# Light expert units loaded behind the next heavy block's units, light stages spaced unevenly, and a small copy moved on

## What is computed

```
def _swiglu(h, w_gate, w_up, w_down):
    return (jax.nn.silu(h @ w_gate) * (h @ w_up)) @ w_down

def _moe(h, router, w_gate, w_up, w_down):
    logits = (xf @ router).astype(jnp.float32)
    top_logits, top_idx = lax.top_k(logits, TOP_K)
    gates = jax.nn.softmax(top_logits, axis=-1)
    ...  # each expert: _swiglu of its tokens, with w_gate[e], w_up[e], w_down[e]
    ...  # the results, times their gates, are summed by token
```

## Time and profile before

| what | value |
|---|---|
| median of 3 runs | 1554.77 us (1552.6 to 1555.14) |
| profiled execution: time, span in the trace | 1556.36 us, 1554.6 us |
| busy time in the span: PE, DVE, ACT, POOL | 95%, 58%, 47%, 20% |
| DMA: bytes, mean rate over the span | 469.61 MB, 302 GB/s |
| rate in the slices of the MoE | mostly 350 to 409 GB/s |

### The profile page before, as it was taken

One profiled execution on the slowest core, in us unless ns is written; L12 is line 12 of the kernel. 1 busy time (PEld: TensorE's weight loads), 2 busy tenths in 40 slices (PEclk: granted clock), 3 DMA queues, 4 the chain that ended last, 5 costly groups with the idle time before them and its releaser, 6 DMA issues.

```text
span 1554.6 us, 22445 instructions
## 1 busy us (share of the span) xinstructions
PE 1482.5 (95%) x9550; PEld 1138.3 (73%) x9550; DVE 907.6 (58%) x665; ACT 731.7 (47%) x588; POOL 303.4 (20%) x295
## 2 busy tenths in 40 slices
PE   9999999999999999999999999999998999999997
PEld 8887889999988788876565565666655666656675
DVE  5555566655567748865454555554554545545687
ACT  5444445433355356753444445444444444444565
POOL 5599225300035205840000000000000000000100
PEclk9999999999999999999999999999999999999999
DMA  9544548765521186998999999999999999999994
GB/s 346 177 163 162 190 158 290 275 214 181 186 79 57 44 321 225 374 381 354 406 370 407 361 392 409 371 398 397 382 392 379 409 349 385 395 376 396 390 381 160
DMA packets 141598, 469.61 MB, mean 302 GB/s; under 512 B 8649, under 2 KB 21153, under 8 KB 129201
## 3 DMA queue, kind: packets, MB, share of 16 engines
q1 hardware_dynamic: 137424, 454.58, 77.3%
q0 software_dynamic: 3920, 13.44, 2.6%
q10 hardware_dynamic: 144, 0.07, 0.0%
HBM read 462.02 MB, written 15.21 MB: 307 GB/s over the span
## 4 chain that ended last, share of the span: by engine, by line
PE 66%; DMA 16%; DVE 8%; ACT 7%; issue 2%; POOL 1%; SPq 0%; ACTq 0%; DVEq 0%; POOLq 0%
PE PS L2037 64%; DMA weights_raw<-in_moe_w_up 6%; DMA weights_raw<-in_moe_w_down 6%; ACT weights_hi L1111 6%; DVE weights_lo L1531 6%; DMA weights_raw<-in_moe_w_gate 3%; PE PS L2252 1%; POOL b_padded L929 1%; PE PS L2451 0%; ACT c_padded L1111 0%; DVE act_rows L1531 0%; DVE residual L1531 0%; POOL param_tmp L788 0%; DMA constants<-in_constants 0%; DVE small_act_rows L1531 0%
## 5 line engine op out<-in xcount | busy, mean ns | idle before, releaser
L1531 DVE TENSOR_TENSOR weights_lo<-weights_raw,weights_hi 128x2048 fp32r<-128x2048 f32 (+2 forms) x323 | 680.0, 2114 | 527.7 <-ACT weights_hi L1111 526.4
L1111 ACT ACTIVATE weights_hi<-weights_raw 128x2048 fp32r<-128x2048 f32 (+2 forms) x323 | 564.0, 1752 | 576.3 <-PE PS L2037 218.7
L2037 PE MATMUL PS<-weights_hi,gathered_hi 128*128 128x512 f32 (+1 forms) x640 | 241.8, 378 | 33.6 <-DVE weights_lo L1531 33.0
L2037 PE MATMUL PS<-weights_lo,gathered_hi 128*128 128x512 f32 (+1 forms) x640 | 234.2, 366 | 0.0
L2037 PE MATMUL PS<-weights_hi,gathered_lo 128*128 128x512 f32 (+1 forms) x640 | 234.1, 366 | 0.0
L2037 PE MATMUL PS<-weights_hi,act_transposed_hi 128*128 128x512 f32 x456 | 187.8, 412 | 13.5 <-DVE weights_lo L1531 13.4
L2037 PEld LDWEIGHTS PS<-weights_hi,gathered_hi 128*128 128x128 f32 x640 | 120.1, 188 | 88.8 <-issue 40.9
L2037 PE MATMUL PS<-x_transposed_hi,weights_hi 128*128 128x256 f32 x640 | 181.2, 283 | 1.3 <-DVE weights_lo L1531 1.1
L2037 PE MATMUL PS<-weights_hi,act_transposed_lo 128*128 128x512 f32 x456 | 181.6, 398 | 0.0
L2037 PE MATMUL PS<-weights_lo,act_transposed_hi 128*128 128x512 f32 x456 | 181.5, 398 | 0.0
L2037 PE MATMUL PS<-x_transposed_lo,weights_hi 128*128 128x256 f32 x640 | 179.7, 281 | 0.0
(11 more groups left out here) (330 smaller groups left out, 1453.8 us busy)
## 6 DMA issues: line engine op xcount, KB each, us to landing
weights_raw<-in_moe_w_up SPq DMA_DIRECT2D x127, 896.0 KB, 9.0
weights_raw<-in_moe_w_gate SPq DMA_DIRECT2D x125, 896.0 KB, 8.8
weights_raw<-in_moe_w_down SPq DMA_DIRECT2D x96, 1024.0 KB, 8.1
weights_raw<-in_ret_w_in SPq DMA_DIRECT2D x24, 1024.0 KB, 6.7
weights_raw<-in_moe_w_down SPq DMA_DIRECT2D x32, 512.0 KB, 7.7
weights_raw<-in_ffn_w_gate SPq DMA_DIRECT2D x14, 1024.0 KB, 5.1
weights_raw<-in_ffn_w_up SPq DMA_DIRECT2D x14, 1024.0 KB, 5.0
weights_raw<-in_ffn_w_down SPq DMA_DIRECT2D x14, 1024.0 KB, 4.9
```

Source lines behind the costliest of these rows:

```text
L1111: return nc.scalar.activation(o, i, ACT.Copy)
L1531: return nc.vector.tensor_tensor(o, a, b, op)
L2037: return nc.tensor.matmul(o, l, r, start=start, stop=stop)
```

## The change

`small_after` now reads a table in which each light stage has its own places: four blocks behind four heavy blocks in a row, one heavy block with none, then the two down blocks. Behind every second stage there is one more heavy block with none. `units_in_order` takes the number of blocks by which light units are loaded behind their place of use: 1 for loading (`ORDER`, `NUMBER`), 0 for use (`USED_ORDER`). In the load order the units of the light block of place k now follow those of heavy block k + 1; TensorE still uses them ahead of that heavy block. `done_at(n)` gives the value of `used` at which load number n was used, and takes the place of `n + 1` in all waits on `used` in the MoE. On ScalarE the copy to `act_t_small` leaves `after_small` for `after_small_turn`, which runs at l = 2k + 6 instead of 2k + 4.

```
-    turn, at = divmod(k - START, 5)
-    j = 4 * turn + at
-    return j if at < 4 and 0 <= j < len(LIGHT) * len(BLOCKS) else None
+def small_positions():
+    after, k = {}, START
+    for stage in range(len(LIGHT) * ESTEPS):
+        for at in range(6):
+            after[k] = 6 * stage + at
+            k += 2 if at == 3 else 1
+        k += stage % 2
+    return after
...
-def units_in_order():
+def units_in_order(behind):
...
-        for ranks, at in ((WHOLE, k), (LIGHT, small_after(k))):
+        for ranks, at in ((WHOLE, k), (LIGHT, small_after(k - behind))):
...
+ORDER = units_in_order(1)
+USED_ORDER = units_in_order(0)
+DONE = {NUMBER[of]: MOE_U0 + m + 1 for m, of in enumerate(USED_ORDER)}
+def done_at(n):
+    return DONE.get(n, n + 1)
...
 (SP, load)
-                            sp.wait_ge(used, last + 1)
+                            sp.wait_ge(used, done_at(last))
...
 (ScalarE, split_hi)
-                    act.wait_ge(used, count(SPLIT_UNITS[SPLIT_NUMBER[n] - SPLIT] + 1, e, EXPERT_UNITS))
+                    act.wait_ge(used, count(done_at(SPLIT_UNITS[SPLIT_NUMBER[n] - SPLIT]), e, EXPERT_UNITS))
...
 (ScalarE, after_small)
-                elif kind == "up" and part:
-                    act.wait_ge(turned_small, done + 1)
-                    copy(act_t_small[:, :, :], PS[:, 6, 0:HALF_EC].rearrange("p (f c) -> p f c", f=EFT)).then_inc(act_small_ready, 1)
...
+            def after_small_turn(j):
+                q, b = block_of(LIGHT, j)
+                kind, s, part = SMALL_BLOCKS[b]
+                if kind == "up" and part:
+                    act.wait_ge(turned_small, ESTEPS * LIGHT.index(q) + s + 1)
+                    copy(act_t_small[:, :, :], PS[:, 6, 0:HALF_EC].rearrange("p (f c) -> p f c", f=EFT)).then_inc(act_small_ready, 1)
...
 (ScalarE, first_pass)
+                        j = small_after((l - 6) // 2) if l % 2 == 0 else None
+                        if j is not None:
+                            after_small_turn(j)
```

More of the change, by code:

```diff
@@ L82 @@
 TURNS = (FIRST, 1, 4, 2, 5, 6, 3, 7)
+def small_positions():
[6 more added lines that the diff above has]
+    return after
+SMALL_AFTER = small_positions()
 def small_after(k):
-    turn, at = divmod(k - START, 5)
-    j = 4 * turn + at
-    return j if at < 4 and 0 <= j < len(LIGHT) * len(BLOCKS) else None
+    return SMALL_AFTER.get(k)
 def block_of(ranks, k):
@@ L1196, in expert_work @@
                     s = s0 + silu_at[i]
-                    act.wait_ge(used, count(number(expert_first(silu_at[i]) + 3) + 1, e, EXPERT_UNITS))
+                    act.wait_ge(used, count(done_at(number(expert_first(silu_at[i]) + 3)), e, EXPERT_UNITS))
                     act.wait_ge(mult_done, count(s, e, ESTEPS))
@@ L1433, in after_small @@
                 if kind == "gate" and part:
-                    act.wait_ge(used, NUMBER[q, 2 * b + 1] + 1)
+                    act.wait_ge(used, done_at(NUMBER[q, 2 * b + 1]))
                     if done:
@@ L1444, in after_small @@
                     elif part:
-                        act.wait_ge(used, NUMBER[q, EXPERT_UNITS - 1] + 1)
+                        act.wait_ge(used, done_at(NUMBER[q, EXPERT_UNITS - 1]))
                         if q > LIGHT[0]:
@@ L1457, in first_pass @@
                         if i == 2 and at:
[L1458 removed]
+                            y_out(done_at(NUMBER[WHOLE[at - 1], EXPERT_UNITS - 1]), at - 1 if at > 1 else None)
                         if i == EXPERT_UNITS - 2 and q != LAST:
@@ L1625, in expert_work @@
                     dve.wait_ge(silu_done, count(s + 1, e, ESTEPS))
-                    dve.wait_ge(used, count(number(expert_first(mult_at[i]) + 7) + 1, e, EXPERT_UNITS))
+                    dve.wait_ge(used, count(done_at(number(expert_first(mult_at[i]) + 7)), e, EXPERT_UNITS))
                     if s > STEPS:
@@ L1946, in after_small @@
                     dve.wait_ge(silu_small, ESTEPS * LIGHT.index(q) + s + 1)
-                    dve.wait_ge(used, NUMBER[q, 2 * b + 1] + 1)
+                    dve.wait_ge(used, done_at(NUMBER[q, 2 * b + 1]))
                     tt(act_small[:, :], act_small[:, :], PS[:, 6, 0:HALF_EC], ALU.mult).then_inc(mult_small, 1)
@@ L1957, in first_pass @@
                         if i == 2 and at:
-                            y_out(NUMBER[WHOLE[at - 1], EXPERT_UNITS - 1] + 1, at - 1 if at > 1 else None)
+                            y_out(done_at(NUMBER[WHOLE[at - 1], EXPERT_UNITS - 1]), at - 1 if at > 1 else None)
                         if i == 9 and at == 0:
```

1 line of the change is left out of this document (removed).

## The result

The changed kernel takes 1516.81 us (1516.48 to 1518.12, median of 4) against 1554.24 us in the same comparison: ratio 0.9759, 95% interval 0.9747 to 0.9772. That is 37 us less, where the forecast had 24.

The account below looks back on a forecast made before the run. TensorE and the DMA engines were both taken as near their limits. 27.9 us gained less 4 us of cost gave 24 us, from 1556.4 to 1532.4; with the median 1.6 us lower, 1531 us, range 1513 to 1551.

Parts of the forecast that it names:

- all lulls go: Rival: DMA lulls between 685 and 1458 us all vanish, 44 us, giving 1511 us (1509 to 1519); chance 0.08.
- The lulls: 14 places between 685 and 1458 us where DMA runs under 408 GB/s as the buffer ring is full; 44.3 us.
- Part 1: Light loads behind the next heavy block's: shortest lead 2.2 us longer, taken at each of 14 lulls, 27.9 us gained.
- the reserve: How early loads are issued in paired blocks: shortest lead from 7.5 to 9.75 us, against 9.0 from issue to landing.
- Part 3: Small ScalarE copy one block later: four blocked splits of about 1.65 us go, 6.6 us, not added to the sum.
- Part 4: New places of light blocks: costs up to 8.4 us at six places, taken as half, 4 us.
- the runs of six: Six places where two down blocks meet four more light ones; each takes 1.4 us more of the reserve.
- Part 2: Waits of SP, ScalarE and VectorE name the new count of used; same events for heavy and light units, no cost.
- The small gain: Rival: new spacing makes lulls grow as the lead does, only four blocked splits go; 1548 us, chance 0.27.
- no change: Rival: DMA's bytes alone set the end, so the time stays at 1554.8 us; chance 0.07.
- The slower rival: Light units arrive 4.5 us later and lose their reserve; TensorE waits at landings, 8.4 us more, 1563 us; chance 0.08.
- What would show it: Signs between 685 and 1458 us: some 24 us shorter, 395 to 400 GB/s, fewer lulls, at most 3.5 us each.

Follow-up runs that it names:

- halved kernel: Two-tile light units load only their first tile (light results wrong): 1538.3 us against the kernel before with its old order, 1493.4 us against the changed kernel.
- two-blocks run: The changed kernel with light units loaded two heavy blocks behind their place of use instead of one: 1941.3 us (one run).
- wider spread: The changed kernel with light blocks from k = 14 to 108, behind three of each four heavy blocks, copy half a block earlier, returning rows added later: 1519.7 us.
- order_only: The kernel before with the new load order alone, old spacing and old place of the small copy: 1535.0 us, ratio 0.9867.

## Why the prediction was right, and where it wasn't

**Direction and range** held: 1516.8 us lies in 1513 to 1551, by 3.8 us. It doesn't lie in the forecast's own 1519 to 1543 but in the interval of the rival "all lulls go" (1509 to 1519), to which I gave 0.08. That the range held is in part luck: the sum was 13 us short.

**The lulls as the store of the gain: right as a bound, not as the cause.** Lost DMA time was put at 44 us of the stretch; (1 - 405/408) x 737 is 5.4 us now. But this is no second proof. The bytes are the same, so any shorter stretch has a higher rate. What speaks on the cause is the halved kernel: 28.7 of the 50.4 us of waits stay in the old order when the DMA engines have less to do. The limit of about 358 GB/s that the Trainium skill gives ("DMA: Bandwidth & Descriptors", Where 436 GB/s comes from) doesn't bind this kernel, which runs on one core: 405 GB/s over 737 us.

**Part 1, 27.9 us for the order: too small, and by a wrong step.** The order alone gave 20 us, and 42 to 44 us with the copy out of its way and the old spacing (ratios 0.9731 and 0.9719). Two things failed. First, the size of the reserve. I followed a pair with DMA setting the pace, found 2.2 us more lead, and said that in this state nothing is won. The halved loads showed that the old order waits with the DMA engines not full: the term is the time from issue to need, for the heavy unit behind a light one 6.15 us against 8.6 us to land. Second, I let a heavy unit be split as it lands and give up its buffer after 3.75 us, in the new order too. There the split buffers bind: ScalarE waits 103.8 us in 66 times for TensorE's use of an earlier heavy unit, where it was 15.6 us in 11.

**Part 3, the copy, not added: wrong.** It was to be contained in part 1. It is worth 30 us in the new order over the new spacing, 17 in the old. Over the old spacing it is worth 21 to 23 us in the new order (0.9867 to 0.9731 or 0.9719) and 11 in the old. I had seen the split queued behind the waiting copy, but not the load queued behind the split: SP's waits on weights_lo rose from 197.7 us to 514.6 us, so in the new order the split is the gate of the ring. Over the old spacing, 9.5 us of the 21.8 are waits for landings that went with the copy.

**Part 4, the spacing: right.** I took 4 us of cost, 3.7 us were measured, and in the runs of six. That the old copy place would cost 20 us over the new spacing was right for TensorE's own waits (18.1 us), and short of the 30 us that it cost.

**Part 2,** the new counts of used, could not be told apart from the rest and shows nowhere.

**The rivals.** The small gain (1548) and no change fall with the time, 1516.8 us; the largest lull, 5.5 us in a window before, is 1.4 us (380 GB/s). The slower rival had a true premise: light units have no reserve now, TensorE waits at their landings 31 times. But they are 0.6 us in the mean and 1.8 at most. The two-blocks run shows where it would decide.

**What would show it:** rate 395 to 400 (405 came), waits turned into landings (so it was), ScalarE's wait ahead of the small copy gone (58.4 us before; none in the stretch after), the load queue's 410 us on TensorE down to 57.7.

## What to carry to other kernels

In a ring with loads in order, count for each kind of unit the time from the release of its buffer to its need, less what must be done to it first, and hold that against the measured time from issue to landing under load. Here it paid to load the units that must be prepared ahead of those that are used as they land, even though they are used later, by one step; two steps cost 424 us. Count again before each shift. When the order changes, look at which engine now frees the buffers and clear the waits ahead of that step in its queue: here the two edits together were worth 42 to 44 us over the old spacing, and one by one 20 and 11. The changed kernel still has such a wait: 68.3 us of ScalarE ahead of the turned rows of heavy experts. What it costs wasn't tried.

## What the hardware showed

TensorE's clock fell after some short waits. In the kernel before TensorE stood 2.60 us ahead of the turning at 719.43 (its timeline), and in the windows view the granted clock is 0.66 and then 0.91:

```profile
719.43 1.90 PE L2037 MATMUL PS<-constants,small_act_rows 64*64 64x64 f32 x28 [2.60 <-DVE small_act_rows L1531]
```

```profile
719.00:723.00 4.00, 3.57 (x32) 3.16 (x33) 0.38 (x1) 1.62 (x2) 0.00 (x0) 0.66 1.03 422
723.00:727.00 4.00, 4.00 (x20) 3.36 (x20) 3.25 (x2) 3.20 (x3) 0.00 (x0) 0.91 0.25 102
```

That is a loss of 4 x 0.34 + 4 x 0.09 = 1.7 us of full-speed time, with part of the stretch at the lower level of 1.2 GHz. The same followed the wait of 2.58 us ahead of 1245 (0.91 over 1240 to 1260) and the longest wait behind the stretch, 2.69 us. The length of the wait alone doesn't tell: after the wait of 2.48 us that began at 1179 the clock stayed at 1.00. In the halved old order it fell after one of 2.34 us, and in the wider spread it stayed at 1.00 after one of 3.53 us:

```profile
1168.60 0.62 PE L2040 MATMUL PS<-constants,small_act_rows 64*64 64x64 f32 x6 [2.34 <-DVE small_act_rows L1534]
```

```profile
1168.00:1172.00 4.00, 3.40 (x32) 3.00 (x33) 0.55 (x2) 1.46 (x2) 0.00 (x0) 0.58 0.98 397
```

```profile
1473.98 0.47 PE L2060 MATMUL PS<-weights_hi,gathered_hi 128*128 128x512 f32 x1 [3.53 <-DVE weights_lo L1554]
```

```profile
1474.00:1478.00 4.00, 4.00 (x20) 3.56 (x21) 4.00 (x3) 1.25 (x1) 0.00 (x0) 1.00 1.01 384
```

The changed kernel has no such drop ahead of its end. The two drops in the stretch before cost 3.4 us by this count, and TensorE's work there fell by 3.5 us. That the one is the other isn't shown: order_only has no drop in its stretch either, and is busy 723.3 us there. The prediction had no term for it.

The time from issue to landing of a unit was 8.6 us in the median of the kernel before, and 9.6 after the change, though at 408 GB/s a unit of 896 KB takes 2.25 us of the DMA engines. By my estimate from these numbers some four units are under way at a time (9.6 / 2.25), and a lead is to be held against the 9.6 us and not the 2.25.
